# One vector-engine step moved behind the tile work beside it, and its 48 loads moved from GpSimd's queue to SyncE's

## The reference

```python
def swiglu(u, w_gate_up, w_down):
    gate, up = jnp.split(u @ w_gate_up, 2, axis=-1)
    return (jax.nn.silu(gate) * up) @ w_down

# in the second block, for both layers:
    mod = c_act @ ada_w[layer] + ada_b[layer]      # 1024 -> 3 * 1024
    shift, scale, gate = jnp.split(mod, 3, axis=-1)
```

## Time and profile before

| | us |
|---|---|
| median of 3 runs (lowest, highest) | 3027.36 (3026.05, 3027.86) |
| the profiled execution's own time | 3027.36 |
| its span, from first to last instruction | 3025.5 |
| PE busy | 2891.0 (96%) |
| DVE busy | 1731.7 (57%) |
| ACT busy | 1243.9 (41%) |
| POOL busy | 423.2 (14%) |

### The profile page before, as it was taken

The page is one execution under the profiler, slowest core; times in us unless marked ns, Lnnn a source line. Parts: engine busy times, 40 slices in busy tenths (PEclk is TensorE's granted clock), DMA queues, the critical chain, the costliest instruction groups (busy, mean ns, idle before and its releaser), DMA issues.

```text
span 3025.5 us, 37063 instructions
## 1 busy us (share of the span) xinstructions
PE 2891.0 (96%) x14578; PEld 2413.6 (80%) x14578; DVE 1731.7 (57%) x2258; ACT 1243.9 (41%) x2028; POOL 423.2 (14%) x352
## 2 busy tenths in 40 slices
PE   8999998899999999999999999998999899999998
PEld 6877886687888888888888777787888787888976
DVE  6564476663554444444444745688888835317874
ACT  5221456332443111111112335577767724427851
POOL 0000005200000000000000000255544300004520
PEclk9999999999999999999999999999999999999999
DMA  4111334032222233322331222100001212131031
GB/s 145 56 42 50 126 105 184 26 118 84 91 63 72 73 91 98 92 81 75 87 93 42 76 88 63 56 1 5 15 15 39 98 59 88 49 91 57 22 112 70
DMA packets 226587, 219.28 MB, mean 72 GB/s; under 512 B 9456, under 2 KB 195056, under 8 KB 224880
## 3 DMA queue, kind: packets, MB, share of 16 engines
q1 hardware_dynamic: 214752, 174.90, 18.5%
q0 software_dynamic: 6912, 25.17, 2.8%
q10 hardware_dynamic: 4752, 16.84, 1.5%
HBM read 180.12 MB, written 34.67 MB: 71 GB/s over the span
## 4 chain that ended last, share of the span: by engine, by line
PE 86%; DVE 7%; ACT 3%; issue 2%; POOL 2%; DMA 0%; SPq 0%; ACTq 0%; DVEq 0%; POOLq 0%
PE P L342 61%; PE P L280 5%; PE P L2409 3%; PE P L311 2%; POOL T L2669 2%; PE P L283 1%; PE P L285 1%; PE P L284 1%; PE P L2423 1%; PE P L1104 1%; PE P L2422 1%; DVE PTL L1517 1%; DVE WST L2648 1%; PE P L3010 1%; PE P L1552 1%
## 5 line engine op out<-in xcount | busy, mean ns | idle before, releaser
L267 DVE TENSOR_TENSOR wl<-wf,wh 128x1024 fp32r<-128x1024 f32 (+4 forms) x239 | 251.6, 1053 | 923.8 <-ACT wh L259 923.5
L259 ACT ACTIVATE wh<-wf 128x1024 fp32r<-128x1024 f32 (+4 forms) x239 | 219.8, 920 | 1030.1 <-PE P L342 985.6
L342 PE MATMUL P<-AQ,wh 128*128 128x512 f32 x1824 | 489.4, 390 | 5.8 <-issue 3.0
L342 PE MATMUL P<-XH,wh 128*128 128x512 f32 (+1 forms) x1264 | 396.1, 395 | 8.9 <-DVE XL L1346 5.2
L342 PEld LDWEIGHTS P<-AQ,wh 128*128 128x128 f32 x1824 | 341.3, 188 | 77.9 <-issue 4.6
L342 PE MATMUL P<-XL,wh 128*128 128x512 f32 (+1 forms) x1264 | 391.2, 391 | 0.0
L342 PE MATMUL P<-XH,wl 128*128 128x512 f32 (+1 forms) x1264 | 391.2, 391 | 0.0
L2669 POOL TENSOR_TENSOR T<-T,WST 128x1024 f32<-128x1024 f32 x128 | 242.6, 1895 | 573.8 <-DVE WST L2641 573.8
L342 PEld LDWEIGHTS P<-XH,wh 128*128 128x128 f32 (+1 forms) x1264 | 235.7, 187 | 65.5 <-issue 14.6
L342 PE MATMUL P<-AQ,wl 128*128 128x512 f32 x912 | 280.8, 389 | 0.0
L342 PEld LDWEIGHTS P<-XL,wh 128*128 128x128 f32 (+1 forms) x1264 | 236.2, 187 | 52.6
(11 more groups left out here) (438 smaller groups left out, 5006.2 us busy)
## 6 DMA issues: line engine op xcount, KB each, us to landing
AW<-ada_w POOLq DMA_DIRECT2D x48, 512.0 KB, 4.1
wf<-w_gate_up SPq DMA_DIRECT2D x44, 512.0 KB, 3.8
H<-scratch_h SPq DMA_DIRECT2D x32, 512.0 KB, 6.5
wf<-w_in SPq DMA_DIRECT2D x28, 512.0 KB, 3.8
scratch_h<-H SPq DMA_DIRECT2D x24, 512.0 KB, 5.7
scratch_g<-T ACTq DMA_DIRECT2D x22, 512.0 KB, 3.0
wf<-odd_w_in SPq DMA_DIRECT2D x20, 512.0 KB, 3.8
wf<-even_w_in SPq DMA_DIRECT2D x17, 512.0 KB, 3.8
```

What stands on the lines that cost most here:

```text
L259: e.activation(self.sb["wh"][i % 2][:, 0:m], self.sb["wf"][i % 2][:, 0:m], ACT.Copy).then_inc(*self.s.w_hi.up(i))
L267: e.tensor_tensor(l, f, h.bitcast(F32), ALU.subtract).then_inc(*self.s.w_lo.up(i))
L342: ins = e.matmul(self.P[slot][0:m, t:t1], w, x[:, k, t:t1], start=first and k == 0, stop=last and k == kb - 1)
```

## The change

The 48 loads of `AW` leave POOL's queue and stand in SP's, between the weight loads: the first two ahead of the stage's own weight loads, behind a wait for the last tile of the stage before, and the load for step n+2 behind the weight load of the tile that has step n. In DVE's queue the step stands behind the tile's own work (product, gate, low part, or the addition to `H`), no longer ahead of it. The distribution of steps over tiles, the place of the sums in PE's queue and all sizes stay.

```diff
-    def pool_ada(self, e, n):
+    def sp_ada(self, e, n):
         if n < 48:
             layer, part, k = self.ada(n)
             if n > 1:
...
     def sp_ffn(self, e):
-        for stage, j, _, _ in self.ffn_tiles():
+        e.wait_ge(*self.s.mm.to(("wo", 7)))
+        self.sp_ada(e, 0)
+        self.sp_ada(e, 1)
+        for stage, j, step, _ in self.ffn_tiles():
             if (stage, j) in self.last_of:
                 self.sp_weights(e, self.last_of[stage, j] + 4)
+            if step is not None:
+                self.sp_ada(e, step + 2)
         self.sp_weights(e, self.no["va", 0] + 1)
-
-    def pool_ffn(self, e):
-
-        e.wait_ge(*self.s.mm.to(("wo", 7)))
-        for n in range(48):
-            self.pool_ada(e, n)
...
             def empty(e, j):
+                for i in (j,) if n else {0: (), 1: (0, 1)}.get(j, (j,)):
+                    product(e, i)
                 if plan[("gu", n), j][0] is not None:
                     self.dve_ada(e, plan[("gu", n), j][0])
-                for i in (j,) if n else {0: (), 1: (0, 1)}.get(j, (j,)):
-                    product(e, i)
...
             def empty(e, j):
+                add(e, n, j)
                 if plan[("dn", n), j][0] is not None:
                     self.dve_ada(e, plan[("dn", n), j][0])
-                add(e, n, j)
             return empty
...
     def gpsimd(self, e):
         self.pool_ssd(e)
-        self.pool_ffn(e)
         self.pool_attention(e)
         self.pool_windowed(e)
```

## The result

The changed kernel took 3049.94 us (median of 4 runs, 3049.18 to 3051.33) against 3026.70 of the kernel before (4 runs). The ratio is 1.0078, with a 95% interval from 1.0060 to 1.0095. It is 23 us slower, where 8 were forecast and 3038.6 us was the upper end of the range. The direction and the first mechanism were right. The size was not, because of a term that had been set to nothing.

The account below looks back on a forecast made before the run. PE was taken to bound the kernel, so only added PE waits count. +4.5 - 0.2 + 0.7 + 3.1 = +8.1 us on 3027.36 gave 3035.5 us, 0.27% slower, range 3032.2 to 3038.6.

Parts of the forecast that it names:

- What bounds it: From 930 to 1660 us the chain of waits runs on PE almost throughout; tile matmuls are 97.9% of it.
- Sum 0, +4.5 less 0.2: Behind dn0[0], PE waits for the later step 7, +4.5 us; a little comes back in dn0, -0.2.
- sum 1, +0.7: Behind dn1[5], PE waits for step 15, which now starts where the addition ended: +0.7 us (0.5 to 0.9).
- The four other sums: They stand behind a gu tile, 10.9 us after the one with the step, so they don't wait: 0.
- The clock, +3.1: After the new idle at sum 0, half clock costs the sum 1.7 us and 3 us of tiles 1.4.
- Tiles and pairs, 0: In the stage's tiles and PSUM pairs, the product comes one step earlier, which PE doesn't need: 0.
- the wait of 2.0 us at dn1 stays: PE's one wait, after gu2, ends with a wl behind the same operations in another order: change 0.
- The loads, 0: At the start and in the stage, AW loads and held weight loads in SP's queue make PE wait 0.
- a new wait for a weight load stands in PE's list: A stated sign, in the profile after, that the prediction is wrong; no size given.
- The rival of loads in one queue: Each weight load behind an AW load is late by its landing less the slack: 3036.5 to 3038.5 us, 8%.
- The taking of turns: DMA engines alternate between GpSimd's queue and the ring; on this footing the late slab at dn1[4] was counted 0.
- 4.8 to 5.3: The us range given for the waits of sum 0 and sum 1, less what comes back.

Follow-up runs that it names:

- the filler: The changed DVE order with AW loads left in POOL's queue, plus 16 unread matmuls ahead of sum 0 in PE's queue: 3032.93 us against 3026.94 before.
- the weights first: The changed kernel with each AW load of the stage behind the next weight load in SP's queue: 3037.00 us against 3026.94 for the kernel before.
- the SP half alone: The kernel before with AW loads moved to SP's queue and DVE's order left as it was: 3030.64 us against 3027.70.
- The long hold without it: The changed kernel with POOL issuing AW again, while SP still waits in its queue for step n: 3039.97 us against 3027.70 for the kernel before.
- the DVE half alone: The kernel before with steps behind the tile's work on DVE and AW loads left in POOL's queue: 3037.45 us against 3027.70.

## Why the prediction was wrong, by its own steps

- **What bounds it:** right. PE's queue is the path, and only what makes PE wait counts.
- **Sum 0, +4.5 less 0.2, sum 1, +0.7:** right. The idle stretch was 4.41 us, the step started 5.15 us behind its tile's `wl` (1042.83 to 1047.98) where it had been 0.34, so 4.81 later, as the pitches gave, and sum 1 idled 0.73. With the clock held up by the filler the stage was +5.1, for 5.0 in the forecast. The four other sums, and the start of the stage, cost nothing, as was said.
- **The clock, +3.1:** close for the place that it was worked out for (3.0 in the table, 3.3 by the filler run), in part by luck: the sum lost 1.0 where 1.7 were taken, and the tiles 2.0 where 1.4 were. For the kernel it was short, because more idle stretches came that the forecast did not have, and the clock fell at two more places. 8.0 in all.
- **Tiles and pairs, 0; the wait of 2.0 us at dn1 stays:** right; it is in every run with DVE's new order, and in the kernel before.
- **The loads, 0: this step failed.** The text says of SP's queue that the next weight load "waits for a `wl` which DVE only makes after step n". It doesn't. The section on the kernel says that SP waits for the `wl` of the slab after next and loads the slab four after the tile's; the bound in `sp_weights` is exclusive, so it is the `wl` of the next slab and the load three after. The next load in SP's queue, ahead of which the change put the wait for step n, waits for a `wl` that is the first thing DVE makes at this very tile. In the kernel before the trace had it: `wl` ended 1044.79, and this row of SP, of the kernel before, comes right behind it and ahead of the end of step 7 at 1045.99:

```profile
1044.82 0.37 SPq L250 DMA_DIRECT2D wf<-w_down  x1
```

  The changed kernel at the end of gu2, from its timeline:

```profile
1143.95 0.42 DVE L267 TENSOR_TENSOR wl<-wf,wh 128x256 fp32r<-128x256 f32 x1 [8.12 <-ACT wh L259]
...
1150.41 0.34 SPq L1698 DMA_DIRECT2D AW<-ada_w  x1
...
1150.80 5.10 SPq L250 DMA_DIRECT2D wf<-w_down  x3
```

  The load was free to go at 1144.4 and went at 1150.80, 6.4 us late, behind the whole DVE chain of the tile. At the start of a down stage the tiles are short, and with the late landing that is more than the slack. What the runs showed in place of the 0 is 6.9 us of waits for weights, and, with what came with them, 13 us of the time (3049.94 against 3037.00 with the weights first). The prediction had named the sign: it is wrong "if a new wait for a weight load stands in PE's list".
- **The rival of loads in one queue** was a right mechanism at the wrong places and with too little chance (8%). It was priced for dn1[4] and on the footing that SP issued on time. Standing behind `AW` adds 1.6 us to a small load (3.8 and 2.2) and 1.2 to a big one (5.0 and 3.8). Without the hold that is hidden: with the weights first, no tile waits for a weight, though six down loads landed late; with a hold of one step (the SP half alone) it cost 1.5 us. The long hold without it is nearly hidden: 0.9 us. Both together are not: 6.9 us of waits at six places. Neither could be priced without the other, since each used up the slack that hid the other.
- **What the rule was worth.** The Trainium skill's order within a ring ("DMA: Bandwidth & Descriptors", section "Queues, rings and completion order") was weighed and set to 0. Within SP's queue this case's runs agree with it: behind `AW` the slab took 3.8 us, ahead of it 2.2. The taking of turns, for which the prediction set 0, did not spare a load that came 0.20 us behind an `AW` of POOL's queue: 192 KB took 4.5 to 5.6 us there, in place of 2.4. The 2.2 us beside POOL's `AW` were those of a load that went out 0.3 us ahead of it.
- **The range:** its "4.8 to 5.3" for the two sums doesn't follow from the bounds given for them, which make 4.6 to 5.5. The measured time lies far outside by either.

What stays open: the 1.7 us of remainder were not taken apart further. That the clock falls behind a wait of 2.0 us in some executions and not in others was seen, and not explained. And no run had the held weight go out behind an `AW` of POOL's queue; the late loads of the run with the DVE half alone suggest that it would have come late there too.

## What to carry to other kernels

A transfer moved into the queue of another engine brings its wait with it, and everything behind it is held for that long: read, for each instruction now behind it, what it waited for before and at what time that came true in the trace, and do it from the rows of the queue itself, not from a reading of the loop's bounds. Issue what is already free to go ahead of what has to wait, and small loads ahead of big ones. A sum or any short piece that waits for another engine's last step belongs a tile behind that step or into a gap that exists anyway; taking such a piece out of its gap costs as much as it did.

## What the runs showed of the hardware that I had not expected

- A small load is late by its place behind a big one, not by the bytes in flight: 128 KB took 2.2 us when issued 0.3 to 0.4 us ahead of 512 KB, of its own queue or of POOL's, and 3.8 when issued 0.4 behind them in its own queue. Behind 512 KB of POOL's queue, by 0.20 us, 192 KB took 4.5 to 5.6 in place of 2.4; by 0.07 us, 128 KB took 2.2 to 2.9.
- The granted clock fell to 0.50 behind idle stretches of PE of only 2.0 us in the profiled executions of four of these kernels, and not in seven others with the same wait. Behind 4.4 us it fell in all six profiles that have such a stretch, for 6.8 us, which cost 3.3 us of the time.
- The one-column sum, early in which the clock fell, took 2.9 us in place of 1.7.
